# Gated output of the RWKV heads in even steps 0 to 6: from VectorE to GpSimd and ScalarE

## The reference

```python
p = h @ even_w_in[j]
a_out = diff_attention(p[..., :3 * DA_WIDTH], ...)
b_out = rwkv7_time_mix(p[..., 3 * DA_WIDTH:], ...)
mix = jnp.concatenate([a_out, b_out], axis=-1) @ even_w_out[j]
```

```python
yn = ((y - mean) * lax.rsqrt(var + RW_GN_EPS)) * ln_w + ln_b
bonus = jnp.sum(r_h * k_h * r_k, axis=-1, keepdims=True) * v_h
return ((yn + bonus) * g)
```

## Time and profile before

| | us |
|---|---|
| timed runs, median (lowest to highest) | 2507.18 (2506.55 to 2507.42) |
| the profiled execution | 2504.34 |
| its span | 2502.5 |
| PE busy in the span | 2474.1 (99%) |
| DVE busy | 1852.5 (74%) |
| ACT busy | 1224.1 (49%) |
| POOL busy | 490.9 (20%) |

### The profile page before, as it was taken

How to read it: one execution, slowest core, us unless ns; L and a number is a source line. 1 busy time by engine, 2 the same in 40 slices (tenths; PEclk the granted TensorE clock), 3 DMA queues, 4 the chain that set the end, 5 groups by cost and what they waited for, 6 DMA issues and landing times.

```text
span 2502.5 us, 47792 instructions
## 1 busy us (share of the span) xinstructions
PE 2474.1 (99%) x17536; PEld 2187.6 (87%) x17536; DVE 1852.5 (74%) x3043; ACT 1224.1 (49%) x1753; POOL 490.9 (20%) x407
## 2 busy tenths in 40 slices
PE   8999999999999999999999999999999999999998
PEld 8899998888888888888888888888888888888887
DVE  7898889776665666566989999997666556655665
ACT  6555565554433444334656565655444434443444
POOL 1222222122200221022212212113222012200220
PEclk9999999999999999999999999999999999999999
DMA  7333332445555555555554444446455555555553
GB/s 272 117 126 134 124 121 108 164 180 190 186 194 191 184 184 196 190 185 179 178 203 163 168 157 175 154 154 222 179 185 186 200 187 185 198 192 185 194 191 128
DMA packets 65576, 438.43 MB, mean 175 GB/s; under 512 B 9408, under 2 KB 10816, under 8 KB 15808
## 3 DMA queue, kind: packets, MB, share of 16 engines
q1 hardware_dynamic: 61632, 436.29, 48.6%
q10 hardware_dynamic: 3840, 0.70, 0.1%
HBM read 434.87 MB, written 2.10 MB: 175 GB/s over the span
## 4 chain that ended last, share of the span: by engine, by line
PE 83%; DVE 8%; issue 4%; ACT 3%; POOL 1%; DMA 0%; ACTq 0%; DVEq 0%; SPq 0%; POOLq 0%
PE acc L332 24%; PE acc L402 17%; PE mixer_banks L413 9%; PE acc L384 9%; PE acc L396 9%; PE acc L367 5%; PE acc L329 5%; DVE w_low L322 2%; DVE arena L1534 2%; ACT L955 1%; DVE arena L445 1%; DVE arena L1522 1%; POOL arena L607 1%; DVE arena L1524 1%; PE mixer_banks L1656 1%
## 5 line engine op out<-in xcount | busy, mean ns | idle before, releaser
L317 ACT ACTIVATE w_high<-w_raw 128x1024 fp32r<-128x1024 f32 x831 | 862.5, 1057 | 871.7 <-PE acc L384 388.6
L322 DVE TENSOR_TENSOR w_low<-w_raw,w_high 128x1024 fp32r<-128x1024 f32 x832 | 1055.8, 1296 | 119.8 <-ACT w_high L317 117.3
L332 PE MATMUL acc<-h_split,w_high 128*128 128x512 f32 x2688 | 670.9, 393 | 1.1
L332 PEld LDWEIGHTS acc<-h_split,w_high 128*128 128x128 f32 x2688 | 491.7, 188 | 99.4 <-DVE arena L445 3.1
L562 POOL TENSOR_TENSOR arena<-arena,norm_scale 128x256 f32<-128x256 f32 x152 | 224.5, 1477 | 1355.7 <-DVE arena L445 1336.0
L445 DVE TENSOR_REDUCE arena<-acc 128x256 f32<-128x512 f32 x254 | 174.7, 688 | 288.0 <-PE acc L402 178.2
L402 PE MATMUL acc<-h_split,w_high 128*128 128x512 f32 x1376 | 328.2, 391 | 0.0
L402 PEld LDWEIGHTS acc<-h_split,w_high 128*128 128x128 f32 x1376 | 252.9, 188 | 48.9
L367 PE MATMUL acc<-h_split,w_low 128*128 128x256 f32 x1824 | 274.9, 282 | 0.0
L367 PEld LDWEIGHTS acc<-h_split,w_low 128*128 128x128 f32 x1824 | 255.5, 190 | 15.1
L332 PE MATMUL acc<-mix_split,w_high 128*128 128x512 f32 x752 | 185.1, 393 | 2.6 <-DVE mix_split L1147 2.3
(11 more groups left out here) (322 smaller groups left out, 2415.1 us busy)
## 6 DMA issues: line engine op xcount, KB each, us to landing
w_raw<-w_gu SPq DMA_DIRECT2D x176, 1024.0 KB, 4.8
w_raw<-w_odd SPq DMA_DIRECT2D x64, 1024.0 KB, 4.7
w_raw<-w_even SPq DMA_DIRECT2D x49, 1024.0 KB, 4.8
w_raw<-w_last SPq DMA_DIRECT2D x44, 1024.0 KB, 4.8
w_raw<-w_down SPq DMA_DIRECT2D x32, 1024.0 KB, 4.9
w_raw<-w_down SPq DMA_DIRECT2D x16, 768.0 KB, 4.2
w_raw<-w_odd_out SPq DMA_DIRECT2D x12, 1024.0 KB, 4.8
w_raw<-w_even_out SPq DMA_DIRECT2D x10, 1024.0 KB, 4.8
```

The lines of the kernel that those rows point to most:

```text
L317: act.activation(wh[:, self.res, ks], raw[:, self.raw, ks], ACT.Copy).then_inc(high_done, 1)
L322: dve.tensor_tensor(wl[:, self.res, ks], raw[:, self.raw, ks], wh[:, self.res, ks].bitcast(F32), ALU.subtract).then_inc(low_done, 1)
L332: pe.matmul(acc[self.acc][:, 0:2 * T], wh[:, self.res, k], flat(both), start=k == 0, stop=stop)
```

## The change

For j = 0 to 6 the gated output leaves VectorE. GpSimd adds `bv` and multiplies by `gT`, both in place in `yT`; ScalarE copies `yT` with rounding into the high part; GpSimd subtracts it into the low part and gives `rw_end`. GpSimd does this (`output(j - 1)`) behind `turn(j, 1)` in steps 1 to 6, and ahead of `turn(7, 1)` in step 7. ScalarE's copy (`output_rounded`) stands between `high(3)` and `high(4)` in steps 1 to 6, and ahead of `high(3)` in step 7. VectorE gets one wait more, ahead of the product that overwrites `bv`. The output of j = 7 stays on VectorE. One semaphore of the attention (`at_nb`) is merged into another (`at_mx`), with the same order as before.

```diff
@@ GpSimd
+            def output(j):
+
+                waits(pool, j + 1, "rw_yTs", "rw_bv")
+                pool.tensor_tensor(yT, yT, bv, ALU.add).then_inc(S["rw_out"], 1)
+                pool.wait_ge(S["rw_out"], 2 * j + 1)
+                pool.wait_ge(S["rw_gs"], j + 1)
+                pool.tensor_tensor(yT, yT, gT, ALU.mult).then_inc(S["rw_out"], 1)
+                pool.wait_ge(S["rw_out"], 2 * j + 2)
+                pool.wait_ge(S["rw_rounded"], j + 1)
...
+                pool.tensor_tensor(rest, yT, rounded.bitcast(F32), ALU.subtract).then_inc(S["rw_end"], 1)
...
                 low_part(rn)
-                turn(j, 1)
+                if more:
+                    turn(j, 1)
+                if not isinstance(j, int) or j > 0:
+                    output(j - 1)
+                if not more:
+                    turn(j, 1)
@@ ScalarE
+            def output_rounded(j):
+
+                act.wait_ge(S["rw_out"], 2 * j + 2)
+                act.activation(mh[:, NRW + j], yT, ACT.Copy).then_inc(S["rw_rounded"], 1)
...
                 if j > 0:
                     late_loads(j)
+                if j > 0 and not more:
+                    output_rounded(j - 1)
                 high(3)
+                if j > 0 and more:
+                    output_rounded(j - 1)
                 high(4)
@@ VectorE
                 evacuate(-1)
                 if j == 0:
                     low(2)
-                if not more:
-                    gated(j - 1)
-                    rounded(j - 1)
...
                     shifts(j + 1)
                     swap(j + 1, 0)
-                    if j > 0:
-                        gated(j - 1)
                 dve.wait_ge(S["rw_y"], j + 1)
...
                 dve.wait_ge(S["rw_bonus"], j + 1)
+                if j > 0:
+                    dve.wait_ge(S["rw_out"], 2 * j)
                 dve.tensor_tensor(bv, bank(0)[:, 0:T], xm[:, 2], ALU.mult).then_inc(S["rw_bv"], 1)
-                if more and j > 0:
-                    rounded(j - 1)
                 dve.wait_ge(S["rw_ysq"], j + 1)
```

More of the change, by code:

```diff
@@ L281, in build @@
             "rw_S rw_S0 rw_R1 rw_nR1 rw_U1 rw_Us1 rw_y rw_ymean rw_yc rw_ysq rw_yvar rw_yln rw_yrs rw_yn rw_yT rw_yTs",
-            "rw_g rw_gs rw_out rw_end rw_scaled",
-            "at_rot at_sin at_cos at_qk at_s at_sm at_mx at_nb at_p at_rc at_w at_wT at_wt at_vT at_vn at_o at_ss at_ln",
+            "rw_g rw_gs rw_rounded rw_out rw_end rw_scaled",
+            "at_rot at_sin at_cos at_qk at_s at_sm at_mx at_p at_rc at_w at_wT at_wt at_vT at_vn at_o at_ss at_ln",
             "at_rs at_on at_oT at_out at_end",
@@ L575, in low_part @@
                 pool.tensor_tensor(parts[:, 1], whole, parts[:, 0].bitcast(F32), ALU.subtract).then_inc(S["rw_suml"], 1)
+            def output(j):
[6 more added lines that the diff above has]
+                pool.wait_ge(S["rw_rounded"], j + 1)
+                rounded = mh[:, NRW + j] if isinstance(j, int) else mh[:, bass.ds(j + NRW, 1)].rearrange("p a t -> p (a t)")
+                rest = ml[:, NRW + j] if isinstance(j, int) else ml[:, bass.ds(j + NRW, 1)].rearrange("p a t -> p (a t)")
+                pool.tensor_tensor(rest, yT, rounded.bitcast(F32), ALU.subtract).then_inc(S["rw_end"], 1)
             def turn(j, c):
@@ L764, in even_step @@
                 z_copy(2)
-                act.wait_ge(S["at_nb"], j + 1)
+                act.wait_ge(S["at_mx"], 3 * j + 3)
                 for q, cols in enumerate((slice(0, P), slice(P, 3 * P))):
@@ L1137, in gated @@
                 dve.tensor_tensor(yT, yT, bv, ALU.add).then_inc(S["rw_out"], 1)
-                dve.wait_ge(S["rw_out"], 3 * j + 1)
+                dve.wait_ge(S["rw_out"], 2 * j + 1)
                 dve.wait_ge(S["rw_gs"], j + 1)
@@ L1142, in rounded @@
             def rounded(j):
-                dve.wait_ge(S["rw_out"], 3 * j + 2)
+                dve.wait_ge(S["rw_out"], 2 * j + 2)
                 dve.tensor_scalar(mh[:, NRW + j], otmp, 1.0, None, ALU.mult).then_inc(S["rw_out"], 1)
-                dve.wait_ge(S["rw_out"], 3 * j + 3)
+                dve.wait_ge(S["rw_out"], 2 * j + 3)
                 dve.tensor_tensor(ml[:, NRW + j], otmp, mh[:, NRW + j].bitcast(F32), ALU.subtract).then_inc(S["rw_end"], 1)
@@ L1270, in even_step @@
                 dve.reduce_max(amx[:, 2:4], prob[:, :, P:3 * P], AX.X).then_inc(S["at_mx"], 1)
-                dve.wait_ge(S["at_mx"], 2 * j + 2)
-                dve.tensor_scalar(anb, amx, -0.125, None, ALU.mult).then_inc(S["at_nb"], 1)
+                dve.wait_ge(S["at_mx"], 3 * j + 2)
+                dve.tensor_scalar(anb, amx, -0.125, None, ALU.mult).then_inc(S["at_mx"], 1)
                 def bonus_factors():
```

## The result

The changed kernel takes 2513.14 us in the median of 10 runs (2511.80 to 2514.07), the kernel before 2506.61 us in 10 runs beside it (2504.28 to 2507.42): ratio 1.0027, 95% interval 1.0018 to 1.0035, so +6.5 us where +7.8 was forecast. The profiled executions lie further apart, 2504.34 and 2513.98 us (spans 2502.5 and 2512.1, +9.6).

| stretch of the span | before | after | difference |
|---|---|---|---|
| up to the start of step 0 | 59.69 | 61.01 | +1.3 |
| step 0 | 51.21 | 51.19 | 0 |
| steps 1 to 6 | 307.27 | 311.19 | +3.9 |
| step 7 up to line 1711 (after: 1733) | 11.50 | 15.60 | +4.1 |
| from there to the end | 2072.8 | 2073.1 | +0.3 |

A forecast was written before the change was run, and what follows sets the result against it. TensorE was taken as the bound. Removal 0, steps 1 to 6 +6.3 and step 7 +1.5 made +7.8 us, a median of 2515.0 us (own range 2508.5 to 2519.1; 8 in 10: 2507.5 to 2519.5).

The forecast's parts named there:

- The removal: Lines taken from VectorE at the end of steps 1 to 6: savings fall into idle time, taken as 0.
- GpSimd's operations hold VectorE up: Steps 1 to 6: three added operations delay VectorE through shared SBUF ports, 1.05 us a step, 6.3 us in all.
- a slack of 0.45: Steps 1 to 6: 0.45 us between VectorE's line 1208 ending and TensorE starting line 1711, subtracted from the delay.
- the cost of one operation: Steps 1 to 6: each added GpSimd operation was taken to delay VectorE by 0.50 us, three per step.
- four places: Trace spots where VectorE and GpSimd share SBUF, read as two-operand VectorE operations losing 0.42 to 0.70 us per GpSimd operation.
- the pair at line 322: Two `low` operations beside two GpSimd operations: 3.83 us against 2 x 1.22, read as 0.70 lost for each.
- Step 7: the wait: Step 7: the remainder comes later through ScalarE's queued rounding, lengthening TensorE's wait by 1.5 us (1.3 to 2.0).
- Slack: Rival: slack covers VectorE's delay in steps 1 to 6, leaving mainly step 7; about 2509.5 us, chance 0.24.
- whole instructions: Rival: each added GpSimd operation costs VectorE its full 0.74 us in steps 1 to 6; 2519.3 us, chance 0.10.
- second loss: Rival: VectorE's delay continues past line 1208, TensorE waits again at line 1747; 2520.7 us, chance 0.05.
- The relief of VectorE: Rival: step 7's 2.28 us wait and line 1311's 1.3 us of waits go; 2503.6 us, chance 0.05.

The follow-up runs named there:

- e8: Kernel before without the gated output of j = 0 to 6, those tiles zeros: the removal by itself; 2503.22 us, ratio 0.9986.
- e5: Kernel before plus three unused GpSimd sums of constants in each of steps 1 to 6, nothing removed; 2510.61 us, ratio 1.0018.
- e7: Kernel of e3 with GpSimd's sum, product, remainder and ScalarE's rounding placed later within steps 1 to 6; 2502.39 us, ratio 0.9988.
- e3: Changed kernel with ScalarE's rounding in step 7 moved ahead of the exponentials; 2507.17 us, ratio 1.0003 against the kernel before.
- e6: Like e5, but the three added GpSimd operations only fill a tile with zeros, reading no SBUF; 2506.38 us, ratio 0.9999.
- e4: Kernel before with only step 7's output of j = 6 on GpSimd and ScalarE, rounding ahead of the exponentials; 2503.72 us, ratio 0.9987.
- e1: Kernel before with only step 7's output of j = 6 moved, placed as in the changed kernel; 2507.03 us, ratio 1.0002.
- e2: Changed kernel with the output of j = 6 back on VectorE, so only steps 1 to 6 changed; 2508.95 us, ratio 1.0010.

## Why the prediction was right, and where its sizes were off

**The removal pays nothing in steps 1 to 6: right, and shown.** e8 takes the lines away without any replacement and its steps stay at 51.2 us.

**GpSimd's operations hold VectorE up at the start of the step, past a slack of 0.45: right, and shown** by e5 (the loss without the rest of the change) and e7 (no loss in another place). The mis-sized term is the cost of one operation: 0.50 was taken, the trace shows 0.39 for the sum (1.52 against 1.13 for the two scans), 0.25 for the product and 0.45 for the remainder, 1.1 us in place of 1.5. Less the slack that is 0.65 to 0.73 a step, not 1.05: 3.9 us in place of 6.3. An average per operation was the wrong unit. The traces hold a closer one, the part of GpSimd's operation that is still to run when VectorE's begins (step 5 of each; "longer" is against the shortest of the same line; L443 is from 55.17 us of its trace):

| VectorE's operation | GpSimd's still to run, us | longer, us |
|---|---|---|
| scaling L1167 (before) | 0.68 | 0.54 |
| first scan L1171 (before) | 0.54 | 0.42 |
| second scan L1198, beside the sum (changed) | 0.51 | 0.40 |
| copy L1201, beside the product (changed) | 0.40 | 0.26 |
| L1229, beside the remainder (changed) | 0.59 | 0.45 |
| L1217, beside the third sum (e5) | 0.57 | 0.43 |
| L443, one operand in PSUM (before) | 0.68 | 0.01 |
| L1281, one operand in PSUM (e7) | 0.42 | 0.01 |
| shuffle L1112 (before) | 0.67 | 0.01 |
| reduction L1348 (before) | 0.54 | 0.00 |

In the first six rows VectorE loses what is still to run, less 0.11 to 0.15 us; in the last four it loses nothing. No run varied this by itself, so it is a reading of rows. It also corrects two readings of the prediction. Its four places were not all operations with two operands in SBUF: line 1167 has one, and so has line 1201. And the loss of the pair at line 322 is not 0.70 for each: the first kept its time (1.18 us), and the second, which began with 0.58 us of GpSimd's first still to run and all 1.10 of its second ahead, took 2.72 us in place of 1.22.

**Step 7: the wait was right.** +1.40 us where +1.5 was forecast, and e3 shows that ScalarE's place in the chain is the reason: with the rounding moved, the wait is 0.17.

**What the sum lacked: the clock.** No term stood for it. In the two profiles compared it costs 2.7 us in step 7, in the medians less. The runs of the kernel before fall into two groups by their mean granted clock: in its second set of 33, 4 have 0.999 (2503.2 to 2504.5 us; the profiled execution is of this kind) and 29 have 0.998 (2504.8 to 2507.4); in the first set it is 1 and 32. The changed kernel has 0.998 in five runs (median 2512.1) and 0.997 in five (median 2514.0). e5 and e6 show what a short stretch costs: their step 7 is that of the kernel before, with the same wait of 2.28 us, and both have the clock at 0.50 for 3.4 us and reach line 1711's counterpart 13.02 us into the step in place of 11.50, so 1.5 us. If the median run of the kernel before has this stretch, the medians should differ by 3.9 + 1.4 + 2.7 - 1.5 = 6.5 us, which is what was measured. That is an estimate; that the kernel before has it is not shown, since its one profile has none in step 7. Nor is step 7 the only place. Behind it, with the wait of 2.36 us for the remainder of j = 7, eight of the ten profiles have the clock at 0.50 for 3.4 us; e5 and e7 do not, and they take 2030.1 and 2030.4 us from there to the end, the others 2031.1 to 2032.1. So the groups of one kernel can come from either place.

The total, +6.5 for +7.8, was close in part by luck: the mis-sized term (2.4 us too much) and the missing one (about 1.2 us in the medians, by the estimate) cancel in part.

**The rivals.** Slack did not hide the port (steps are longer). VectorE did not lose GpSimd's whole instructions: 1.1 us for three, against 0.64 to 0.75 each. But it did lose nearly all that was left of each. There was no second loss: line 1747's counterpart shows no wait. The relief of VectorE did come in the one place that its rival named, but only once the rounding stood ahead of the exponentials (e3, e4, e7).

## What to carry to other kernels

Moving work off a busy engine pays only where the bounding engine waits for it; look first at what the freed lines stand in front of, since lines that fill a wait are free already. When GpSimd takes over elementwise work, place it beside VectorE's waits or its operations that read PSUM, and read the slack of the next operand in the line, since less than half a microsecond of it decides. When a chain crosses an engine with a long list of its own, one instruction moved up in that list can be worth more than the work moved.

## What the runs showed of the hardware that was not expected

- A `tensor_scalar` on two numbers per partition took 0.42 us when it began beside a GpSimd product, and 0.17 with nothing beside it: even a tiny operation can be held up, by what is left of GpSimd's less 0.11 to 0.15 us (the table above). A VectorE operation that reads PSUM, a shuffle and a reduction kept their time beside 0.42 to 0.68 us of a GpSimd operation.
- TensorE's granted clock was 0.50 for 6.8 us in step 7 with a wait of 3.7 us (changed kernel, e1), for 3.4 us with waits of 2.0 and 2.3 us (e2; e5 and e6), and stayed at 1.00 there with waits of 0.2 us (e3, e4, e7) and, in one profile, with 2.3 us (before). The 6.8 us cost 2.7 us in the changed kernel, the 3.4 us in e5 and e6 cost 1.5: on top of the wait, more than half of it again. Whether it comes with a wait of about 2 us differs from run to run.
